# Bias rows and two norms' sums as two fp32r products each, and three steps of a hybrid attention block in another order

## What is computed

```python
h = rmsnorm(x, norm_attn)                     # x * rsqrt(mean(x^2) + eps) * g
proj = h @ w_in                               # q, k, v, branch gates, stick-breaking qkv, merge gates
o_nsa = nsa_attention(...)                    # 8 heads: compressed, selected, window branch, T5 bias
o_sb = stick_breaking_attention(q, k, v)      # 8 heads; z = q k, log_keep = log_sigmoid(z) - z, summed from the right
mixed = sigmoid(g0) * (o_nsa @ w_up_nsa) + sigmoid(g1) * (o_sb @ w_up_sb)
x = x + mixed @ w_out
h = rmsnorm(x, norm_mlp)
x = x + square(relu(h @ w_ff1)) @ w_ff2
return rmsnorm(x, norm_final)
```

## Time and profile before

| | |
|---|---|
| median of 3 runs | 793.69 us (793.33 to 793.8) |
| profiled execution | 796.9 us |
| its span in the trace | 795.0 us |
| busy: PE, PEld | 782.3 us (98%), 639.5 us (80%) |
| busy: DVE, ACT, POOL | 399.0, 330.3, 357.5 us (50%, 42%, 45%) |
| chain that ended last | PE 95%, DVE 2%, ACT 1%, DMA 1% |
| panels (L1252) in that chain | 69% |

### The profile page before, as it was taken

The page is one execution under the profiler, slowest core; times in us unless marked ns, Lnnn a source line. Parts: engine busy times, 40 slices in busy tenths (PEclk is TensorE's granted clock), DMA queues, the critical chain, the costliest instruction groups (busy, mean ns, idle before and its releaser), DMA issues.

```text
span 795.0 us, 11378 instructions
## 1 busy us (share of the span) xinstructions
PE 782.3 (98%) x3860; PEld 639.5 (80%) x3860; DVE 399.0 (50%) x812; ACT 330.3 (42%) x591; POOL 357.5 (45%) x462
## 2 busy tenths in 40 slices
PE   8999999999999999999999999999999999999996
PEld 6878887887877777778888888888888888888896
DVE  7445556777757676636443375541255114521234
ACT  6333323588966576674343332321232222321221
POOL 1255424511112332146555477665567546655540
PEclk9999999999999999999999999999999999999999
DMA  7954012211150110134233223223233233233213
GB/s 246 333 191 156 1 61 72 88 46 54 23 163 30 53 54 28 54 106 160 79 107 104 92 94 106 85 101 106 83 101 106 81 103 106 79 106 104 82 54 106
DMA packets 25989, 77.59 MB, mean 98 GB/s; under 512 B 3710, under 2 KB 6966, under 8 KB 25695
## 3 DMA queue, kind: packets, MB, share of 16 engines
q1 hardware_dynamic: 23868, 74.72, 28.3%
q10 hardware_dynamic: 2083, 2.37, 1.0%
HBM read 73.90 MB, written 2.13 MB: 96 GB/s over the span
## 4 chain that ended last, share of the span: by engine, by line
PE 95%; DVE 2%; ACT 1%; DMA 1%; issue 0%; ACTq 0%; DVEq 0%
PE bank L1252 69%; PE bank L1563 2%; PE bank L1545 2%; PE bank L1597 2%; PE bank L1602 2%; PE bank L1601 2%; PE bank L1478 2%; PE bank L1523 1%; PE bank L1496 1%; PE bank L1264 1%; PE bank L1265 1%; PE bank L1266 1%; PE bank L1378 1%; PE bank L1529 1%; DMA xs<-in_xT 1%; PE bank L1460 1%
## 5 line engine op out<-in xcount | busy, mean ns | idle before, releaser
L535 POOL TENSOR_TENSOR wlo<-wraw,whi 128x256 fp32r<-128x256 f32 x440 | 342.9, 813 | 395.8 <-ACT whi L576 206.8
L594 ACT ACTIVATE whi<-wraw 128x1024 fp32r<-128x1024 f32 x48 | 51.0, 1062 | 154.7 <-PE bank L1252 150.2
L1252 PE MATMUL bank<-hh,wlo 128*128 128x512 f32 x304 | 82.5, 402 | 0.4 <-DVE gm L1055 0.3
L1252 PE MATMUL bank<-hl,whi 128*128 128x512 f32 x304 | 80.6, 392 | 0.0
L1252 PE MATMUL bank<-hh,whi 128*128 128x512 f32 x304 | 79.6, 391 | 0.0
L1189 DVE TENSOR_TENSOR x_res<-bank,x_res 128x512 f32 (+1 forms) x28 | 19.4, 693 | 117.2 <-PE bank L1252 117.2
L576 ACT ACTIVATE whi<-wraw 128x1024 fp32r<-128x1024 f32 x53 | 55.5, 1052 | 28.0 <-PE bank L1252 19.3
L1252 PEld LDWEIGHTS bank<-hh,wlo 128*128 128x128 f32 x304 | 56.5, 192 | 12.7 <-DVE x_res L1164 0.6
L1252 PEld LDWEIGHTS bank<-hl,whi 128*128 128x128 f32 x304 | 56.5, 188 | 11.8 <-issue 0.2
L1252 PEld LDWEIGHTS bank<-hh,whi 128*128 128x128 f32 x304 | 56.6, 188 | 11.7
L1252 PE MATMUL bank<-h2h,wlo 128*128 128x512 f32 x256 | 65.9, 391 | 0.0
(11 more groups left out here) (253 smaller groups left out, 1214.1 us busy)
## 6 DMA issues: line engine op xcount, KB each, us to landing
wraw<-in_panels SPq DMA_DIRECT2D x113, 512.0 KB, 3.3
w1k<-in_w SPq DMA_DIRECT2D x1, 2048.0 KB, 9.3
w1v<-in_w SPq DMA_DIRECT2D x1, 2048.0 KB, 15.3
svraw<-in_panels SPq DMA_DIRECT2D x4, 512.0 KB, 5.5
hank<-bias_by_distance SPq DMA_DIRECT2D x4, 512.0 KB, 6.3
x_res<-in_xT SPq DMA_DIRECT2D x4, 512.0 KB, 4.5
out_dram<-x_res SPq DMA_DIRECT2D x12, 128.0 KB, 1.8
xs<-in_xT SPq DMA_DIRECT2D x4, 256.0 KB, 7.2
```

The lines of the kernel that those rows point to most:

```text
L535: ins = nc.gpsimd.tensor_tensor(wlo[:, s, k:k + 2], wraw[s][:, k:k + 2], whi[:, s, k:k + 2].bitcast(F32), ALU.subtract)
L594: A(whi[:, s], wraw[s][:], ACT.Copy).then_inc(w_hi, 1)
L1252: ins = M(b[:, cols], lhs, (xl if a == 1 else xh)[:, row + k, cols], start=(m == 0), stop=(m == 23))
```

## The change

Four products in fp32 (the first norm's, the second norm's and the two of the bias rows) become two products each in fp32r: the moving or stationary operand that is not exact is split into its rounded value and the rounded rest. Ones and the one-hot table are exact. ACT makes the rounded values of the two sums and copies the one-hot table, DVE makes the two rests, both parts of the small bias table and the cast of ones. ACT's two copies in the first norm stand ahead of its Ln. Then three steps change their place: the third `cmp_transpose` comes behind the panel i = 4 in place of i = 3; the gate logit of head 0 comes behind the three maxima; `scores(2)` comes ahead of the eight gate products.

```diff
-CMP_TRANSPOSE = [0, 2, 3, 6]
+CMP_TRANSPOSE = [0, 2, 4, 6]
...
+        relx_r = place("relx_r", [BUCKETS + 1, 2, H], F32R, at=at_sbq + 14080)
+        oneh_r = place("oneh_r", [BUCKETS + 1, 2 * T], F32R, at=tmp_at)
+        sqs_r = place("sqs_r", [P, 2, T], F32R, at=at_sbq)
+        ones_r = place("ones_r", [P, P], F32R)
+        x_ss_r = place("x_ss_r", [P, 2, T], F32R, at=at_sbk + 16384 + 2048)
...
+            act.wait_ge(sqs_done, KT)
+            A(sqs_r[:, 0], sqs[:], ACT.Copy).then_inc(sqs_hi, 1)
+            act.wait_ge(table_in, 16 * 3)
+            A(oneh_r[:], oneh[:], ACT.Copy).then_inc(table_hi, 1)
             ps = result(act, "rms")
...
+            act.wait_ge(x_ss, KT)
+            A(x_ss_r[:, 0], mx[0][:], ACT.Copy).then_inc(x_ss_hi, 1)
             ps = result(act, "rms2")
...
+            dve.wait_ge(set_done, 1)
+            V.tensor_copy(ones_r[:], ones[:]).then_inc(set_done, 1)
...
+            dve.wait_ge(sqs_hi, 1)
+            V.tensor_tensor(sqs_r[:, 1], sqs[:], sqs_r[:, 0].bitcast(F32), ALU.subtract).then_inc(sqs_lo, 1)
+            dve.wait_ge(table_in, 16 * 3)
+            dve.wait_ge(set_done, 4)
+            V.tensor_copy(relx_r[:, 0], relx[:]).then_inc(table_lo, 1)
+            dve.wait_ge(table_lo, 1)
+            V.tensor_tensor(relx_r[:, 1], relx[:], relx_r[:, 0].bitcast(F32), ALU.subtract).then_inc(table_lo, 1)
...
-                if h % 2 == 0:
+                if h % 2 == 0 and h:
                     gate_logit(h // 2)
                 for i, lo, hi in SB_A:
                     dve.wait_ge(zl, 3 * h + i + 1)
 
                     V.tensor_tensor(w[:, lo:hi], bank[b + i][:, 0:hi - lo], w[:, lo:hi], ALU.max).then_inc(zs, 1)
+                if h == 0:
+                    gate_logit(0)
...
+            dve.wait_ge(x_ss_hi, 1)
+            V.tensor_tensor(x_ss_r[:, 1], mx[0][:], x_ss_r[:, 0].bitcast(F32), ALU.subtract).then_inc(x_ss_lo, 1)
...
-                pe_.wait_ge(table_in, 16 * 3)
+                pe_.wait_ge(table_hi, 1)
+                pe_.wait_ge(table_lo, 2)
                 b = claim(pe_, f"vec{i}")
-                filled(M(b[0:H, :], relx[:], oneh[:, T * i:T * i + T], start=True, stop=True), f"vec{i}")
+                for part in (1, 0):
+                    ins = M(b[0:H, :], relx_r[:, part], oneh_r[:, T * i:T * i + T], start=(part == 1), stop=(part == 0))
+                filled(ins, f"vec{i}")
...
-            pe_.wait_ge(set_done, 4)
-            pe_.wait_ge(sqs_done, KT)
-            filled(M(b[:], ones[:], sqs[:], start=True, stop=True), "rms")
+            pe_.wait_ge(set_done, 5)
+            pe_.wait_ge(sqs_lo, 1)
+            for part in (1, 0):
+                ins = M(b[:], ones_r[:], sqs_r[:, part], start=(part == 1), stop=(part == 0))
+            filled(ins, "rms")
...
             scores(1)
+            scores(2)
             gate_products(gate_done, NS_AHEAD)
...
-                    if 1 < u < UNITS:
+                    if 2 < u < UNITS:
...
-            pe_.wait_ge(x_ss, KT)
-            filled(M(b[:], ones[:], mx[0][:], start=True, stop=True), "rms2")
+            pe_.wait_ge(x_ss_lo, 1)
+            for part in (1, 0):
+                ins = M(b[:], ones_r[:], x_ss_r[:, part], start=(part == 1), stop=(part == 0))
+            filled(ins, "rms2")
```

More of the change, by code:

```diff
@@ L395, in block_kernel @@
         h_hi, h_lo, sq_done, sqs_done = sem("h_hi"), sem("h_lo"), sem("sq_done"), sem("sqsum_done")
+        table_hi, table_lo, sqs_hi, sqs_lo, x_ss_hi, x_ss_lo = sem("bias_table_hi"), sem("bias_table_lo"), sem("sqsum_hi"), sem("sqsum_lo"), sem("x_sqsum_hi"), sem("x_sqsum_lo")
         rst, gn_split, gate_st = sem("rstd_ready"), sem("gate_weights_split"), sem("branch_gate_steps")
```

## The result

The changed kernel takes 790.19 us (median of 9 runs, 789.28 to 792.31), the kernel before 794.12 in the same comparison (9 runs, 793.33 to 797.39). The ratio is 0.9948 with a 95% interval from 0.9934 to 0.9962, so the change gives 3.9 to 4.1 us. The forecast was 787.3 with a range from 786.3 to 789.2: the sign was right, the gain of 6.35 us was not, and the time lies above the range.

A forecast was written before the change was run, and what follows sets the result against it. TensorE (PE), carrying 95% of the chain, was taken to bound the kernel. Gains of 1.8 + 0.45 + 3.7 + 0.4 = 6.35 us off the median 793.69 gave 787.3, range 786.3 to 789.2.

The forecast's parts named there:

- 1.6 more, at half clock: Eight products behind the c_k wait at the third comparison transposes: 3.44 us where 1.81 is normal, counted as recoverable.
- a fall of the clock: Rival: around head 0 of the changed kernel the clock falls once, costing 1.6 us, giving 788.9; chance 0.1.
- Two rounded products for one: At the start, three fp32 products become six fp32r products, 3.14 us to 1.36: gain 1.8 us.
- The cover: At the start, ACT's and DVE's 2.8 us of rounding steps hide under PE's value products.
- The second norm: The second norm's fp32 product, 0.91 us, becomes 0.45: gain 0.45 us.
- Transposes and logit together: Third comparison transposes and head 0's gate logit moved: PE's wait exit at L1460 comes 3.7 us earlier.
- the logit's move: Head 0's gate logit behind the three maxima: the chain gains 0.7 to 0.8 us, cancelling DVE's 0.8 lag.
- my 0.15 for a weight copy: ACT weight copy in the way of DVE's evacuation chain before head 0's softplus, put at 0.15 us.
- The fourth block's transposes: Moved transposes find their input just in time: codes end at 143.9, PE arrives at 144.1.
- The wait on gm: New PE wait of 0.8 us at the 12 gate products, using idle time before L1460, so not added.
- scores(2): Score pair ahead of the gate products fills PE's wait for the gate logit: gain 0.4 us, bounds 0.3 and 0.45.
- The DMA rival: Token DMAs make L1378 wait up to 0.5 us; with the narrow-products rival, 787.8 to 788.5, chance 0.1.

The follow-up runs named there:

- wait filled: Kernel before with eight extra products ahead of the third comparison transposes: 794.16 us; with six warm-up products at the start as well: 793.39 us.
- the run with the bias pairs together: Changed kernel with six warm-up products at TensorE's first waits, plus the second bias pair moved directly behind the first (banks changed too): 788.72 us.
- the kernel with its start filled: Changed kernel plus six extra warm-up products between TensorE's first four real products: 788.71 us, ratio 0.993.
- The transposes alone: Kernel before with only the third comparison transposes moved behind panel i = 4: 791.78 us, ratio 0.9972.
- before with its start filled: Kernel before plus the six extra warm-up products at TensorE's first waits, nothing of the change: 793.43 us.
- rounding alone: Changed kernel without its three moves, so the kernel before with only the two-product bias rows and norm sums: 793.95 us, ratio 0.9987.
- third score pair alone: Kernel before with only the third pair of score products moved ahead of the gate products: 794.85 us, ratio 1.0002.

## Why the prediction was wrong

What makes the traces comparable is the distance from the first norm's product to the end of the span: it repeats within 0.06 us for one kernel and clock. With spans given to 0.1 us it is 767.46 for before with half clock (three traces: 767.46, 767.45, 767.46), 765.77 and 765.83 without it (wait filled), 761.46 and 761.48 for the changed kernel. The change gives 6.0 us against an execution with half clock and 4.3 against one without.

**The step that failed** is "I work out differences in the profiled execution and take them off the median." The profiled execution took 796.9 us and the median is 793.69. I noted both and did nothing with the 3.2 us between them. By what the runs show they are 1.6 to 1.7 us of half clock behind the c_k wait, and what is left, 1.5 us, is of the size by which the start varies (25.05 to 27.54). In the sum the half clock entered as "1.6 more, at half clock" and from there as "PE comes to the next panel 3.6 to 3.7 us earlier". Without it PE comes 1.97 us earlier, and 787.3 + 1.6 is 788.9, within the range. So the clock is the largest part of the miss, but not all of it. With the traces' 4.3 in place of 6.35 the forecast would have been 789.4, still above the range; of the last 0.8 us to 790.19, 0.4 are a higher median of before in this comparison and 0.4 the difference between 4.3 and the measured 3.9. I had weighed a fall of the clock as a rival for the changed kernel, and never asked whether the fall in the kernel before was in every execution.

**Two rounded products for one.** The mechanism was right, the size was off. Forecast 1.8 us at the start, measured 1.12 to 1.20. Each pair costs 0.55 instead of 0.454, and the 0.3 us behind the pairs (3.14 less three times 0.95), which I called "the change of type behind them", stayed: 8.14 - 6.20 - 1.66 = 0.28. It can't be the type, since the pairs and the products behind them now have one type. It goes with the change of the weights' shape, as the run with the bias pairs together shows. The Trainium skill, FP8 and Floating Point Precision, section TensorE Precision Notes, has fp32 in four passes, which the trace bears out (four pitches of 0.227 are 0.91, and the product takes 0.95 with the change behind it); two passes saved for each of three products would be 1.36 by my pitch, nearer to what was measured than my 1.8. I overruled the page by a difference of two rows that held something else. The cover held where PE's start is late. Where it is early, at 25.5, DVE's rest is ready only 0.15 us ahead of the product (25.41 and 25.56 in the kernel with its start filled), and the stretch is 0.07 longer, 8.21 or 8.22 in place of 8.14 or 8.15.

**The second norm.** Forecast 0.45, measured 0.45.

**Transposes and logit together.** Forecast 3.7. The transposes alone give 2.0 to 2.1 (763.77 against 765.80, and 139.41 against 141.50 at the third head's logits), the logit 0.24. Against the execution with half clock the same point moved from 143.18 to 137.97, and 1.2 of the 5.2 us are the rounding's: 4.0, where 3.7 stood. The total was added up nearly right, for the wrong execution, but its two parts were not. I had the transposes alone bring the third head's logits 2.9 us forward, with VectorE 0.8 behind PE, and the logit's move give the 0.8 back. The run with the transposes alone moves them by 3.8 (143.18 to 139.41) against half clock. VectorE does lag, by 0.7 at the clamps (3.1 against 3.8; no run shows my 0.15 for a weight copy), but the gate logit ahead of the maxima waits for PE, and that wait, 2.10 us before, takes the lag up. The logit's move was to win the same idle time, so 0.24 of its 0.8 were left. Two errors of opposite sign met here, and the 3.7 came near by luck. The fourth block's transposes were just in time, as forecast.

**The wait on gm.** Forecast 0.8, measured 0.53, and the wait on ew went from 0.9 to none.

**scores(2).** Forecast 0.4, bounds 0.3 and 0.45; measured 0.3.

Added up, the parts alone give 1.57 + 2.03 + 0.3 + 0.24 = 4.1, the whole 4.3 by the traces and 3.9 to 4.1 by the medians. Of the 2.05 us between 6.35 and 4.3, 1.4 lie in the transposes and the logit (3.7 against 2.3), 0.6 to 0.7 in the start's pairs, 0.1 in scores(2), and some 0.1 comes back where the parts meet.

**The rivals.** No clock fell after the wait was gone: the windows show 1.00 from 15 to 783 us, and PE's last products end before that. The Trainium skill's section HAM oscillation, in TensorE: Matmul & The Clock Gate, tells of waits of 3 to 5 us that put the array back each time; I read it as if it held for waits of 0.8 and 0.4 us too. The changed kernel's traces, with one of 0.53, do not show it, while the kernel before went to half clock behind a wait of 1.96. The DMA rival was seen once, as told above. The kernel got faster by more than 1.6 us, as the chances had it; the range was too narrow because no bound in it was taken from the 3.2 us between the profiled execution and the median.

## What to carry to other kernels

Before a difference of the trace is taken off a median, ask how far the profiled execution lies from the median and which rows hold that distance; a term that may be part of it, such as half clock behind a wait, is worth its full price only in the executions that have it. Compare kernels by the distance from a fixed instruction to the end, which repeated here to 0.06 us while the start varied by 2.5. Before two moves are given prices of their own, look whether they win the same idle time. A wait that TensorE has in every execution can cost a second time in some of them, so short waits at the start are worth filling with idle products: it gave 1.4 us.

## What the runs showed of the hardware

- The same wait of 1.96 or 1.97 us on PE was followed by 3 to 4 us at half clock in three traces (before twice, before with its start filled) and by none in two (rounding alone, third score pair alone). The 92.6 us of PE's work ahead of it, from the transposes of rstd_b on, were the same in all five, at full clock. The cost is 1.6 us.
- At the start, with waits of 0.2 to 1.5 us behind the warm-up products, 4 to 12 products ran at a pitch of 0.43 us, or none, from one execution to the next. The longest such wait, 1.45 us in the run with the rounding alone, left none. The Trainium skill, TensorE: Matmul & The Clock Gate, section What's actually happening, has the gate's sampling run free of the kernel's start, so that the point of change differs between runs of one kernel. The traces agree: the first record of full clock begins at 5.4 to 6.3 us in five traces without fillers and at 10.5 to 13.7 in four. In none of the five traces with filled waits did one run so.
- The view of the granted clock can mislead at the start: in the profiled execution of before it reads 1.00 over 9 to 14 us, where the products stand 0.43 us apart. The trace's first record of the clock begins at 13.7 us, and the view shows 1.00 where no record stands. The pitch of the products has to be read beside it.

```profile
9.00:14.00 5.00, 5.00 (x13) 1.00 1.06 404
```

- An fp32 product of 512 columns takes 0.95 us of PE with what follows it, and its pair of fp32r products 0.55 at the same places. Behind the second norm, between products of its own shape, the pair takes 0.46 (440.36 to 440.82).
